# Modulation sums as rows in four column quarters, and a prologue with the first weights behind the first chunk

## The chip, the cores and the metric

The kernel runs on one core of one Trainium2 chip. The metric is the device time of one execution in microseconds. TensorE multiplies, VectorE, ScalarE and GpSimd do the elementwise work, and SyncE issues the DMAs. The inputs are float32.

## What is computed

One sample of 512 latent tokens and 256 context tokens, width 1024, goes through two layers. Each layer is half a gated FFN, a mixer (pooling and neighbourhood attention in layer 0, a gated recurrence in layer 1), and half a gated FFN again. Each block's input is normalised and modulated by shift and scale, and its output by a gate. These modulations are one vector of 9 x 1024 for each layer, and they come from a matrix of 1024 x 9216:

```
mx = (silu(c) @ ada_w[i] + ada_b[i])        # for x
mc = (silu(c_ctx) @ ada_w[i] + ada_b[i])    # for the context
x = x + 0.5 * mx[2] * swiglu(modulate(rms_norm(x, norm_g[i, 0]), mx[0], mx[1]),
                             ffn_w_gu[i, 0], ffn_w_down[i, 0])
...                                         # mixer with mx[3..5], second FFN with mx[6..8]
def modulate(h, shift, scale): return h * (1.0 + scale) + shift
def swiglu(h, w_gu, w_down):
    u = h @ w_gu
    return (silu(u[..., :D_FF]) * u[..., D_FF:]) @ w_down      # D_FF = 2816
```

## The kernel before

**Panels.** All activations lie transposed in SBUF, 128 channels on the partitions and T = 768 tokens along the columns. A product goes panel by panel: a panel is 128 output channels, its weights are 8 k-tiles of 128 x 128 (11 in the down products). Each weight and activation is split in a high and a low part; a k-tile is three products of 768 columns, run as six matmuls of 384 columns. SyncE loads a panel to `raw`, ScalarE rounds it to `w_hi` (`high`, L802), GpSimd subtracts it to `w_lo` (`low`, L691), TensorE multiplies (`panel`, L1661). There are two buffers of each, by the panel's parity, and two PSUM pairs, `pA` (pair_a) and `pB` (pair_b). Semaphores tie the engines: `raw_landed`, `hi_done`, `split_ready`, `panel_used`.

**FFN stages.** A stage `gu{f}{h}` makes the gate and the up panel of 11 channel tiles, in tiles of two panels: ScalarE takes SiLU of the gate (L809), VectorE multiplies by the up product (L1136) and splits the result (L1139, L1142). A stage `dn{f}{h}` makes 8 panels in pairs, each added to the residual by VectorE (L1167, `update`). f counts the four FFNs, h their halves. Where a norm follows (dn01, dn11, dn21, dn31), the last two panels are done in halves of the tokens (`tail`), so that the norm's row sums can start.

**Modulation.** The 9216 columns of a layer are cut in pieces of 256, numbered q, two channel tiles t each. Pieces 0 to 7 (shift and scale of the first norm) are made in the prologue. Pieces 8 to 71 are made one by one beside the FFN panels of f = 0 and 1 and of stage dn20: one piece for each tile of a gu stage, one for each pair of a dn stage, 64 in all. For a piece, SyncE loads 1 MB (`load_ada`), VectorE multiplies its 8 k-tiles by the vectors c and c_ctx, one number for each partition (v = 0, 1), and adds them up (`sum_ada`, L1102 and L1106: 16 instructions). What remains is a sum over the 128 partitions. TensorE does it in `use_ada`:

```
for t in range(2):
    for v in range(2):
        last = nc.tensor.matmul(pC[:, 2 * t + v:2 * t + v + 1], ada_sum[:, v, t * P:(t + 1) * P],
                                ones[:, 0:1], start=True, stop=True)
```

The sums are the stationary operand and a column of ones is moved. VectorE then adds the bias to the four columns (`take_ada`, L1120), which gives `mods`.

**Prologue.** SyncE loads x, the context, the small vectors and four chunks of 2 MB of `ada_w` (`load_ada0`; 2 and 0 are the tiles 0 to 3 of scale and shift, 3 and 1 the tiles 4 to 7). TensorE turns x, multiplies each chunk by c with the channels of `cvec_pad` as four stationary quarters of 32 columns (`ada_rows`, L1836), ScalarE copies the rows out (L940), TensorE turns them (`turn_ada`, L1844), and VectorE adds the bias (L1330). After chunks 2 and 0 VectorE and ScalarE make the normalised rows k = 0 to 3 for both halves of the tokens (`scale_rows` L1234, `high_rows` L863, `low_rows` L1245), after chunks 3 and 1 the rows k = 4 to 7. `first_panels` (L1651 to L1653) then makes panels 0 and 1 in the order: pair_a half 0, pair_b half 0, pair_a half 1, pair_b half 1, each over all eight k.

The order on each engine is the order of the code; the values waited for are written out by hand.

## Time and profile before

| what | us |
|---|---|
| median of the three runs (lowest to highest) | 2862.66 (2860.46 to 2863.76) |
| time of the profiled execution | 2863.28 |
| its span, first to last instruction | 2861.3 |
| TensorE busy | 2705.3 (95%) |
| TensorE weight loads busy | 2545.7 (89%) |
| VectorE, ScalarE, GpSimd busy | 1458.5, 783.1, 895.3 |

The profile shows one execution; an engine's busy time is the union of its instructions. A matmul's end is modelled: it is shown as longer than the distance to the next one. Where matmuls follow each other, the distance from start to start is what one costs; where one group of them ends and another begins, the start of the group's last is its end less the length of one.

### The profile page before, as it was taken

The page shows a single profiled execution, that of the slowest core. Times are in us where ns is not written, and L with a number is a line of the kernel's source. Part 1 is how long each engine was busy: PE and PEld are TensorE (multiplying, and loading weights), DVE is VectorE, ACT ScalarE, POOL GpSimd, SP SyncE. Part 2 cuts the span into 40 slices and gives each one's busy share as a digit, 9 for nine tenths or more (in the row PEclk, how much of TensorE's full clock was granted, in tenths as well). Part 3 has the DMA queues.
Part 4 walks back from the last instruction along what each step waited for, and adds up shares of the span by engine and source line. Part 5 has one row for each costly group of instructions (what it writes and reads, how often), then busy time and mean ns, then how long its engine had stood idle before and what let it go on. Part 6 is the DMA issues. An engine that isn't in the chain of part 4 may idle for free.

```text
span 2861.3 us, 40076 instructions
## 1 busy us (share of the span) xinstructions
PE 2705.3 (95%) x15097; PEld 2545.7 (89%) x15097; DVE 1458.5 (51%) x2525; ACT 783.1 (27%) x1053; POOL 895.3 (31%) x365
## 2 busy tenths in 40 slices
PE   5999999999989899999999999999998887899998
PEld 4899999998957899999999999999997775778887
DVE  5565456655463656645666323422247886432233
ACT  3221122212164322111112322111225664332222
POOL 0332232322232223322222223223223443344442
...
GB/s 201 118 117 131 96 108 122 128 83 71 106 35 22 74 115 120 112 102 120 122 109 89 52 66 95 82 66 61 73 46 52 48 48 66 63 95 103 88 104 80
DMA packets 413084, 256.78 MB, mean 90 GB/s; under 512 B 6653, under 2 KB 405846, under 8 KB 413014
## 3 DMA queue, kind: packets, MB, share of 16 engines
...
q14 instruction: 29, 0.24, 0.0%
...
## 4 chain that ended last, share of the span: by engine, by line
PE 53%; issue 28%; DVE 8%; POOL 7%; ACT 4%; DMA 0%; POOLq 0%; SPq 0%; DVEq 0%; ACTq 0%
PE pair_b L1661 24%; PE pair_a L1661 23%; POOL w_lo L691 7%; PE pair_c L1711 1%; DVE decay L1621 1%; DVE h_lo L1245 1%; DVE ada_sums L1106 1%; DVE decay L1619 1%; DVE gate_i L1615 1%; DVE root L1613 1%; ACT decay L1044 1%; ACT root L1046 1%; PE pair_a L1651 1%; PE pair_r L1955 1%; PE pair_c L1937 1%
## 5 line engine op out<-in xcount | busy, mean ns | idle before, releaser
L691 POOL TENSOR_TENSOR w_lo<-raw,w_hi 128x1024 fp32r<-128x1024 f32 (+3 forms) x302 | 827.2, 2740 | 1764.2 <-ACT w_hi L802 1764.2
L802 ACT ACTIVATE w_hi<-raw 128x1024 fp32r<-128x1024 f32 (+3 forms) x302 | 337.2, 1117 | 1284.2 <-PE pair_b L1661 447.5
L1136 DVE TENSOR_TENSOR work_g<-work_s,pair_b 128x768 f32<-128x768 f32 (+1 forms) x88 | 78.1, 888 | 690.2 <-PE pair_b L1661 526.6
L1106 DVE SCALAR_TENSOR_TENSOR ada_sums<-ada_raw,cvec,ada_sums 128x256 f32<-128x256 f32 x896 | 400.0, 519 | 0.0
L1661 PE MATMUL pair_a<-h_hi,w_hi 128*128 128x384 f32 x1312 | 339.8, 339 | 12.7 <-POOL w_lo L691 12.7
L1661 PE MATMUL pair_a<-h_lo,w_hi 128*128 128x384 f32 x1312 | 334.5, 335 | 0.0
L1661 PE MATMUL pair_a<-h_hi,w_lo 128*128 128x384 f32 x1312 | 334.1, 335 | 0.0
L1661 PE MATMUL pair_b<-h_hi,w_hi 128*128 128x384 f32 x1168 | 298.2, 336 | 10.5 <-POOL w_lo L691 10.5
L1661 PE MATMUL pair_b<-h_lo,w_hi 128*128 128x384 f32 x1168 | 297.6, 335 | 0.0
L1661 PE MATMUL pair_b<-h_hi,w_lo 128*128 128x384 f32 x1168 | 297.3, 335 | 0.0
L1661 PEld LDWEIGHTS pair_a<-h_hi,w_hi 128*128 128x128 f32 x1312 | 235.5, 189 | 17.0 <-issue 8.6
L1661 PEld LDWEIGHTS pair_a<-h_lo,w_hi 128*128 128x128 f32 x1312 | 238.5, 189 | 0.0
L1661 PEld LDWEIGHTS pair_a<-h_hi,w_lo 128*128 128x128 f32 x1312 | 238.0, 189 | 0.0
L1661 PEld LDWEIGHTS pair_b<-h_hi,w_hi 128*128 128x128 f32 x1168 | 211.4, 188 | 11.4 <-POOL w_lo L691 11.4
L1661 PEld LDWEIGHTS pair_b<-h_lo,w_hi 128*128 128x128 f32 x1168 | 211.9, 189 | 0.0
L1661 PEld LDWEIGHTS pair_b<-h_hi,w_lo 128*128 128x128 f32 x1168 | 211.9, 189 | 0.0
L1167 DVE SCALAR_TENSOR_TENSOR resid<-pair_b,mod_g,resid 128x512 f32<-128x512 f32 (+3 forms) x74 | 42.2, 602 | 314.5 <-PE pair_b L1661 245.3
L1651 PE MATMUL pair_b<-h_hi,w_hi 128*128 128x512 f32 (+3 forms) x352 | 140.1, 398 | 32.0 <-DVE gelu L1600 31.8
L1142 DVE TENSOR_TENSOR g_lo<-work_g,g_hi 128x768 f32 (+1 forms) x88 | 155.6, 1768 | 10.8
L1652 PE MATMUL pair_b<-h_lo,w_hi 128*128 128x512 f32 (+3 forms) x352 | 138.1, 392 | 0.0
L1653 PE MATMUL pair_b<-h_hi,w_lo 128*128 128x512 f32 (+3 forms) x352 | 137.3, 390 | 0.0
L1651 PE MATMUL pair_a<-h_hi,w_hi 128*128 128x512 f32 (+2 forms) x280 | 113.4, 405 | 20.7 <-DVE h_lo L1245 16.9
...
## 6 DMA issues: line engine op xcount, KB each, us to landing
...
ada_first<-in_ada_w_dram SPq DMA_DIRECT2D x4, 2048.0 KB, 15.0
...
```

The source lines that it names most:

```text
L691: nc.gpsimd.tensor_tensor(wl[:, par, 0:kt * P], raw[:, par, 0:kt * P], wh[:, par, 0:kt * P].bitcast(F32), ALU.subtract).then_inc(split_rea ...
L802: nc.scalar.activation(wh[:, par, 0:kt * P], raw[:, par, 0:kt * P], ACT.Copy).then_inc(hi_done, 1)
L1044: nc.scalar.activation(decay[d][:, :], gate_r[d][:, :], ACT.Exp, bias=rg_scale[:, m:m + 1], scale=rg_scale[:, m:m + 1])
L1046: nc.scalar.activation(root[d][:, :], gate_r[d][:, :], ACT.Tanh, bias=rg_tanh[:, m:m + 1], scale=rg_tanh[:, m:m + 1]).then_inc(decay_done, 1)
L1106: step = nc.vector.scalar_tensor_tensor(out=sums[v], in0=tiles(k), scalar=c_k, in1=sums[v], op0=ALU.mult, op1=ALU.add)
L1136: nc.vector.tensor_tensor(gbuf[:, 0, 0:W], sbuf[:, 0, 0:W], up, ALU.mult)\
L1142: nc.vector.tensor_tensor(gl[:, ds(i, 1), 0:W].rearrange("p o n -> p (o n)"), gbuf[:, 0, 0:W], gh[:, ds(i, 1), 0:W].rearrange("p o n -> p ...
L1167: return nc.vector.scalar_tensor_tensor(out=resid[:, k, a:b], in0=src, scalar=mod_g[:, SITE[name], k, v:v + 1], in1=resid[:, k, a:b], op0= ...
L1651: nc.tensor.matmul(dst, w1, hi, start=start, stop=False)
L1652: nc.tensor.matmul(dst, w1, lo, start=False, stop=False)
L1653: return nc.tensor.matmul(dst, w2, hi, start=False, stop=stop)
L1661: last = nc.tensor.matmul(tokens(ps, a, a + HALF), w, of[:, k, a:a + HALF], start=begins, stop=ends)
```

## The change

**Modulation sums.** TensorE now keeps a 32 x 128 block of PSUM for each of the four (t, v), in the four quarters of pC's partitions. For a piece, VectorE copies 32 columns of `one_hot` (zero but for one column of ones) to `row_hot`, so that the one stands at the piece's place in its group. `use_ada` then takes `row_hot` (32 columns) as the stationary operand and moves the sums (128 columns), which adds the piece's row to the block. Pieces are gathered in six groups (`GROUPS_AT`) of 11, 15, 4, 11, 15 and 8. `begin_group` clears the blocks by four products with zero weights. When a group is whole, VectorE copies the blocks to SBUF (`copy_group`), TensorE transposes them (`turn_group`) and VectorE adds the bias of the whole group (`take_group`). Four groups are turned within the first pair of the next dn stage, one at the end of dn01's tail, one behind dn20's last panel.

**Prologue.** The weights of panels 0 and 1 are loaded behind chunk 2 and split early; GpSimd no longer waits for the rows k = 0 to 3. Chunk 3's rows are copied after half 0 and chunk 1's after row k = 1 of half 1. `opening_panels` makes panels 0 and 1 in the order: for k = 0 to 3, half 0 of pair_a and pair_b, half 1 of both; then the same for k = 4 to 7. Chunk 1's product stands behind the first eight k-tiles, its turn behind the next four.

```
+        GROUPS_AT = [[("gu00", KC)], [("dn00", KD // 2), ("gu01", KC)], [("dn01", KD // 2)], [("gu10", KC)],
+                     [("dn10", KD // 2), ("gu11", KC)], [("dn11", KD // 2), ("dn20", KD // 2)]]
+        GROUP_OF, GROUP_FIRST, GROUP_SIZE = {}, [], []
+        for g, parts in enumerate(GROUPS_AT):
+            GROUP_FIRST.append(ada_first[parts[0][0]])
+            GROUP_SIZE.append(sum(n for _, n in parts))
+            for part, _ in parts:
+                GROUP_OF[part] = g
+        TURNED_IN = {"dn00": 0, "dn01": 1, "dn10": 3, "dn11": 4}
...
-            load_ada0(2)
-            load_ada0(0)
-            load_ada0(3)
                     if p0 == 0:
+                        load_ada0(2)
                         load(0, 0, KD, gu[:, :, 0:P])
                         load(1, 1, KD, gu[:, :, DFF:DFF + P])
+                        load_ada0(0)
+                        load_ada0(3)
                         load_ada0(1)
...
+            nc.gpsimd.memset(one_hot[:, :], 0.0).then_inc(const_done, 1)
+            pool.wait_ge(const_done, 4)
+            nc.gpsimd.memset(one_hot[:, QUAD - 1:QUAD], 1.0).then_inc(const_done, 1)
-            pool.wait_ge(h_ready, KD)
             ffn(0)
...
             copy_ada0(0, pR, 512)
+            high(0)
+            high(1)
             for half in range(2):
                 root_half("in", half)
             copy_ada0(1, pB, 0)
...
             for half in range(2):
                 for k in range(4):
                     high_rows("in", half, k)
-            copy_ada0(2, pB, 512)
-            high(0)
-            high(1)
-            copy_ada0(3, pA, 0)
+                    if half == 1 and k == 1:
+                        copy_ada0(3, pC, 512)
+                if half == 0:
+                    copy_ada0(2, pB, 512)
             act.wait_ge(coef_done, 2)
...
-            def sum_ada(q):
+            def sum_ada(q, name):
 
                 dve.wait_ge(ada_landed, (q - (ADA0 - 1)) * 16)
+                dve.wait_ge(ada_used, q - (ADA0 - 1))
+                nc.vector.tensor_copy(row_hot[:, :], one_hot[:, ds(q - GROUP_FIRST[GROUP_OF[name]], QUAD)]).then_inc(row_chosen, 1)
                 sum_tiles(lambda k: ada_raw[:, k, :], [ada_sum[:, v, :] for v in range(2)], ada_summed, sums_before(q))
 
-            def take_ada(q):
-
-                dve.wait_ge(ada_used, q - (ADA0 - 2))
-                src = pC[:, 0:4].rearrange("p (t v) -> p v t", v=2)
+            def copy_group(g):
+
+                dve.wait_ge(ada_used, ada_seen(GROUP_FIRST[g] + GROUP_SIZE[g] - 1))
+                nc.vector.tensor_copy(mod_rows[:, :], pC[:, 0:P]).then_inc(group_copied, 1)
+
+            def take_group(g):
+
+                q, n = GROUP_FIRST[g], GROUP_SIZE[g]
+                dve.wait_ge(group_turned, g + 1)
+                turned = pC[:, 640:640 + P].rearrange("p (t v j) -> p v t j", v=2, j=QUAD)[:, :, :, QUAD - n:QUAD]
                 for v in range(2):
-                    last = nc.vector.tensor_tensor(mods[:, ds(q * 2, 2), v], src[:, v, :], cols[:, ds(q * 2, 2)], ALU.add)
-                last.then_inc(mods_done, 1)
+                    last = nc.vector.tensor_tensor(mods[:, 2 * q:2 * (q + n), v].rearrange("p (j t) -> p t j", t=2),
+                                                   turned[:, v, :, ::-1],
+                                                   cols[:, 2 * q:2 * (q + n)].rearrange("p (j t) -> p t j", t=2), ALU.add)
+                last.then_inc(mods_done, n)
...
+                if name in TURNED_IN:
+                    sum_ada(q0, name)
+                    copy_group(TURNED_IN[name])
+                    take_group(TURNED_IN[name])
...
+                if name == "dn20":
+                    copy_group(5)
+                    take_group(5)
...
+            def opening_panels(between):
+
+                p = first["gu00"]
+                for ks in (range(4), range(4, KD)):
+                    for half in range(2):
+                        a, b = half_of("in", half)
+                        for r in range(2):
+                            pe.wait_ge(split_ready, p + r + 1)
+                            for k in ks:
+                                pe.wait_ge(h_ready, row_number(0, half, k) + 1)
+                                last = passes(tokens(pair[r], a, b), r, k, hh[:, k, a:b], hl[:, k, a:b], k == 0, k == KD - 1)
+                            if k == KD - 1 and half == 1:
+                                last.then_inc(panel_used, 1)
+                            between(ks[0], half, r)
+
+            def begin_group(g):
+
+                if g == 0:
+                    pe.wait_ge(const_done, 5)
+                else:
+                    pe.wait_ge(group_copied, g)
+                for c in range(4):
+                    nc.tensor.matmul(pC[c * QUAD:(c + 1) * QUAD, 0:P], one_hot[:, QUAD:2 * QUAD], ident[:, :], start=True,
+                                     stop=False, skip_group_check=True)
+
+            def turn_group(g):
+
+                pe.wait_ge(group_copied, g + 1)
+                if g >= 1:
+                    pe.wait_ge(mods_done, ada_seen(GROUP_FIRST[g] - 1))
+                nc.tensor.transpose(pC[:, 640:640 + P], mod_rows[:, :], ident[:, :]).then_inc(group_turned, 1)
+
+            def use_ada(q, name):
 
                 pe.wait_ge(ada_summed, sums_before(q + 1))
-                pe.wait_ge(mods_done, q - (ADA0 - 1))
+                pe.wait_ge(row_chosen, q - (ADA0 - 1))
                 for t in range(2):
                     for v in range(2):
-                        last = nc.tensor.matmul(pC[:, 2 * t + v:2 * t + v + 1], ada_sum[:, v, t * P:(t + 1) * P],
-                                                ones[:, 0:1], start=True, stop=True)
+                        c = 2 * t + v
+                        last = nc.tensor.matmul(pC[c * QUAD:(c + 1) * QUAD, 0:P], row_hot[:, :], ada_sum[:, v, t * P:(t + 1) * P],
+                                                start=False, stop=False, skip_group_check=True)
                 last.then_inc(ada_used, 1)
...
+                        if opening and r == 0:
+                            if name in TURNED_IN:
+                                turn_group(TURNED_IN[name])
+                            if name in GROUP_OF and ada_first[name] == GROUP_FIRST[GROUP_OF[name]]:
+                                begin_group(GROUP_OF[name])
                         if q0 is not None and r == 0:
-                            use_ada(i + q0)
+                            use_ada(i + q0, name)
+
+                if name in TURNED_IN:
+                    two(0, True)
+                    start = 1
+                with pe.Fori(start, KD // 2 - int(name in NORM_AT)) as i:
+                    two(i)
+                if name == "dn20":
+                    turn_group(5)
...
             turn_ada(2, KD + 4)
-            ada_rows(1, pA[:, 0:512])
-            turn_ada(3, 4).then_inc(ada_used, 1)
+
+            def modulation_ends(k0, half, r):
+
+                if (k0, half, r) == (0, 0, 1):
+                    ada_rows(1, pC[:, 512:1024])
+                elif (k0, half, r) == (0, 1, 0):
+                    turn_ada(3, 4).then_inc(ada_used, 1)
+
             pe.wait_ge(cols_done, 1)
             ffn(0, "in")
```

TensorE in the prologue before, from chunk 3's turn to the first rows of panel 0. L1844 is a chunk's turn, L1836 a chunk's product, L1651 to L1653 the three products of a k-tile:

```order
L1844 MATMUL pair_c<-quad_sums,ada_first_rows 128x2 [waits ada0_copied,mods_first]
L1844 MATMUL pair_c<-quad_sums,ada_first_rows 128x2 x3
L1836 MATMUL pair_a<-ada_first,cvec_padded 32x512 [waits ada0_landed1]
L1836 MATMUL pair_a<-ada_first,cvec_padded 32x512 x7
L1844 MATMUL pair_c<-quad_sums,ada_first_rows 128x2 [waits ada0_copied]
L1844 MATMUL pair_c<-quad_sums,ada_first_rows 128x2 x3
L1651 MATMUL pair_a<-h_hi,w_hi 128x384 [waits h_ready,split_ready,cols_done]
L1652 MATMUL pair_a<-h_lo,w_hi 128x384
L1653 MATMUL pair_a<-h_hi,w_lo 128x384
L1651 MATMUL pair_a<-h_hi,w_hi 128x384 [waits h_ready]
L1652 MATMUL pair_a<-h_lo,w_hi 128x384
```

And of the change, from chunk 3's product (L1926) on; L1934 is a turn, L1686 to L1688 a k-tile:

```order
L1926 MATMUL pair_b<-ada_first,cvec_padded 32x512 [waits ada0_landed3]
L1926 MATMUL pair_b<-ada_first,cvec_padded 32x512 x7
L1934 MATMUL pair_c<-quad_sums,ada_first_rows 128x2 [waits ada0_copied,mods_first]
L1934 MATMUL pair_c<-quad_sums,ada_first_rows 128x2 x3
L1686 MATMUL pair_a<-h_hi,w_hi 128x384 [waits h_ready,split_ready,cols_done]
L1687 MATMUL pair_a<-h_lo,w_hi 128x384
L1688 MATMUL pair_a<-h_hi,w_lo 128x384
```

Chunk 3's turn is now followed by panel 0 at once. Chunk 1's product stands further on in the change, behind the k-tiles 0 to 3 of half 0 of both panels:

```order
L1686 MATMUL pair_b<-h_hi,w_hi 128x384 [waits h_ready]
L1687 MATMUL pair_b<-h_lo,w_hi 128x384
L1688 MATMUL pair_b<-h_hi,w_lo 128x384
L1926 MATMUL pair_c<-ada_first,cvec_padded 32x512 [waits ada0_landed1]
L1926 MATMUL pair_c<-ada_first,cvec_padded 32x512 x7
L1686 MATMUL pair_a<-h_hi,w_hi 128x384 [waits h_ready,split_ready]
```

And its turn stands behind the k-tiles 0 to 3 of half 1 of panel 0:

```order
L1686 MATMUL pair_a<-h_hi,w_hi 128x384 [waits h_ready]
L1687 MATMUL pair_a<-h_lo,w_hi 128x384
L1688 MATMUL pair_a<-h_hi,w_lo 128x384
L1934 MATMUL pair_c<-quad_sums,ada_first_rows 128x2 [waits ada0_copied]
L1934 MATMUL pair_c<-quad_sums,ada_first_rows 128x2 x3
L1686 MATMUL pair_b<-h_hi,w_hi 128x384 [waits h_ready,split_ready]
```

Both have moved from ahead of the panels to between their pieces.

ScalarE in the prologue before, from row k = 3 of half 1 on. L863 is a rounded row, L940 the copy of a chunk's rows, L802 the rounding of a panel's weights:

```order
L863 ACTIVATE h_hi<-work_g,mods 128x128 [waits scaled_done]
L863 ACTIVATE h_hi<-work_g,mods 128x256
L863 ACTIVATE h_hi<-work_g,mods 128x128 [waits scaled_done]
L863 ACTIVATE h_hi<-work_g,mods 128x256
L940 ACTIVATE ada_first_rows<-pair_b 128x512 [waits ada0_mm]
L802 ACTIVATE w_hi<-raw 128x1024 [waits raw_landed0]
L802 ACTIVATE w_hi<-raw 128x1024 [waits raw_landed1]
L940 ACTIVATE ada_first_rows<-pair_a 128x512 [waits ada0_mm]
L863 ACTIVATE h_hi<-work_s,mods 128x384 [waits scaled_done,coef_done]
```

And of the change, from the first chunk's copy (L959) to that of chunk 3; L821 rounds weights, L874 is the norm's root, L882 a rounded row:

```order
L959 ACTIVATE ada_first_rows<-pair_r 128x512 [waits ada0_mm]
L821 ACTIVATE w_hi<-raw 128x1024 [waits raw_landed0]
L821 ACTIVATE w_hi<-raw 128x1024 [waits raw_landed1]
L874 ACTIVATE std<-mean_sq 128x3 [waits ms_done] x2
L959 ACTIVATE ada_first_rows<-pair_b 128x512 [waits ada0_mm]
L882 ACTIVATE h_hi<-work_s,mods 128x384 [waits scaled_done,coef_first]
L882 ACTIVATE h_hi<-work_s,mods 128x384 [waits scaled_done]
L882 ACTIVATE h_hi<-work_g,mods 128x384 [waits scaled_done] x2
L959 ACTIVATE ada_first_rows<-pair_b 128x512 [waits ada0_mm]
```

A little further on, in half 1, the copy of chunk 1 (into which pair_c goes) stands between the rows k = 1 and k = 2:

```order
L882 ACTIVATE h_hi<-work_s,mods 128x128 [waits scaled_done]
L882 ACTIVATE h_hi<-work_s,mods 128x256
L959 ACTIVATE ada_first_rows<-pair_c 128x512 [waits ada0_mm]
L882 ACTIVATE h_hi<-work_g,mods 128x128 [waits scaled_done]
L882 ACTIVATE h_hi<-work_g,mods 128x256
```

The weights are rounded ahead of the norm's root, and both copies moved in among the rows of the first four k.

TensorE at the end of tile 1 of stage gu00 before: the end of the up panel, the sums of a piece (L1711), the loop and the next gate panel:

```order
L1661 MATMUL pair_b<-h_hi,w_lo 128x384 x2
L1711 MATMUL pair_c<-ones,ada_sums 128x1 [waits mods_done,ada_summed]
L1711 MATMUL pair_c<-ones,ada_sums 128x1 x3
L1745 UNCONDITIONAL_BRANCH
L1745 ISA
L1722 REGISTER_ALU [waits split_ready]
L1661 MATMUL pair_a<-h_hi,w_hi 128x384 [waits silu_done]
```

And of the change in the middle of the same tile, where a group begins (L1761) and a piece is taken (L1778):

```order
L1696 MATMUL pair_a<-h_hi,w_lo 128x384 x2
L1761 MATMUL pair_c<-ident,one_hot 32x128 [waits const_done]
L1761 MATMUL pair_c<-ident,one_hot 32x128 x3
L1778 MATMUL pair_c<-ada_sums,row_hot 32x128 [waits row_chosen,ada_summed]
L1778 MATMUL pair_c<-ada_sums,row_hot 32x128 x3
L1696 MATMUL pair_b<-h_hi,w_hi 128x384 [waits gate_up_done,split_ready]
```

The four products of a piece have 32 stationary columns and move 128, where they had 128 and moved 1; they wait for `row_chosen` where they waited for `mods_done`.

VectorE at the beginning of stage dn00, of the change (before, L1092's `mod_g` stood first, then the sums, and L1120 after each piece):

```order
L1135 COPY row_hot<-one_hot 128x32 [waits ada_used,ada_landed]
L1123 TENSOR_SCALAR ada_sums<-ada_raw,cvec 128x256 x2
L1127 SCALAR_TENSOR_TENSOR ada_sums<-ada_raw,cvec,ada_sums 128x256 [waits ada_summed] x14
L1141 COPY mod_rows<-pair_c 128x128 [waits ada_used]
L1149 TENSOR_TENSOR mods<-pair_c,cols 128x2x11 [waits group_turned]
L1149 TENSOR_TENSOR mods<-pair_c,cols 128x2x11
L1113 TENSOR_SCALAR mod_g<-mods 128x16 [waits mods_done]
L1196 SCALAR_TENSOR_TENSOR resid<-pair_a,mod_g,resid 128x512 [waits panel_used,coef_done]
```

The copy of the blocks, the bias of the group and `mod_g` moved behind the sums of the stage's first piece.

## Rows read from the trace of the kernel before

**Rows 1.** Page, first part: busy us (share of the span) x instructions.

```profile
PE 2705.3 (95%) x15097; PEld 2545.7 (89%) x15097; DVE 1458.5 (51%) x2525; ACT 783.1 (27%) x1053; POOL 895.3 (31%) x365
```

**Rows 2.** Timeline of ScalarE: start and length us, line, operation, count, [idle before].

```profile
132.64 0.81 ACT L809 ACTIVATE work_s<-pair_a 128x768 f32<-128x768 f32 x1
150.18 0.81 ACT L809 ACTIVATE work_s<-pair_a 128x768 f32<-128x768 f32 x1
1618.85 0.81 ACT L809 ACTIVATE work_s<-pair_a 128x768 f32<-128x768 f32 x1
1635.49 0.81 ACT L809 ACTIVATE work_s<-pair_a 128x768 f32<-128x768 f32 x1
```

**Rows 3.** Timeline of TensorE round one use of modulation sums.

```profile
139.06 0.51 PE L1661 MATMUL pair_b<-h_hi,w_lo 128*128 128x384 f32 x2
139.41 0.95 PE L1711 MATMUL pair_c<-ones,ada_sums 128*128 128x1 f32 x8
140.22 0.59 PE L1661 MATMUL pair_a<-h_hi,w_hi 128*128 128x384 f32 x2
```

**Rows 4.** Modulation sums on TensorE: ns min/median/max; who it waited for.

```profile
L1711 PE MATMUL pair_c<-ones,ada_sums x512: 165/250/271, 88.1 to 1843.0; 128*128 128x1 f32 x171
  DVE ada_sums L1106: 3.3, 5
```

**Rows 5.** Attention's values: one instruction (ns), TensorE's timeline round their beginning and end.

```profile
L1955 PE MATMUL pair_r<-prob_t,v_tokens x192: 272/273/421, 816.9 to 892.6; 128*64 128x128 f32 x192
819.24 0.66 PE L1937 MATMUL pair_c<-ident,prob 128*128 128x128 f32 x4 [0.23 <-DVE prob L1532]
819.83 0.55 PE L1955 MATMUL pair_r<-prob_t,v_slabs 128*64 128x128 f32 x6
892.25 0.66 PE L1955 MATMUL pair_r<-prob_t,v_tokens 128*64 128x128 f32 x8 [0.82 <-ACT prob_t L903]
892.84 0.62 PE L1661 MATMUL pair_a<-h_hi,w_hi 128*128 128x384 f32 x2
893.29 0.35 PE L1661 MATMUL pair_a<-h_lo,w_hi 128*128 128x384 f32 x1
```

**Rows 6.** Timeline of the prologue: TensorE.

```profile
24.80 1.92 PE L1836 MATMUL pair_r<-ada_first,cvec_padded 128*32 128x512 f32 x16
41.01 3.28 PE L1836 MATMUL pair_b<-ada_first,cvec_padded 128*32 128x512 f32 x16
59.24 0.42 PE L1651 MATMUL pair_a<-h_hi,w_hi 128*128 128x384 f32 x1
```

**Rows 7.** Timeline of the prologue: ScalarE and VectorE.

```profile
45.26 0.61 ACT L863 ACTIVATE h_hi<-work_g,mods 128x384 fp32r<-128x384 f32 x1 [0.44 <-DVE work_g L1234]
59.42 0.24 DVE L1330 TENSOR_TENSOR mods<-pair_c,cols 128x8 f32<-128x8 f32 x2 [7.06 <-PE pair_c L1844]
74.09 1.28 ACT L809 ACT_TABLE_LOAD   x1 [4.21 <-PE pair_a L1653]
```

**Rows 8.** Stretches: length, busy us by engine, clock, DMA share, GB/s.

```profile
30.00:43.00 13.00, 13.00 (x64) 8.60 (x68) 3.55 (x16) 1.63 (x5) 0.00 (x0) 0.51 0.80 268
47.50:57.00 9.50, 4.80 (x24) 2.37 (x24) 4.43 (x13) 5.17 (x11) 3.85 (x2) 0.50 0.01 3
```

**Rows 9.** TensorE's first rows of tile 1 in stage gu00.

```profile
79.64 0.62 PE L1661 MATMUL pair_a<-h_hi,w_hi 128*128 128x384 f32 x2 [1.49 <-POOL w_lo L691]
```

**Rows 10.** Chunk 2: its issue on SyncE's queue; KB and us to landing.

```profile
6.32 8.35 SPq L511 DMA_DIRECT2D ada_first<-in_ada_w_dram  x3
ada_first<-in_ada_w_dram SPq DMA_DIRECT2D x1, 2048.0 KB, 11.9
```

**Rows 11.** Stage dn00, first pair: VectorE, TensorE. Stage dn20: last update.

```profile
268.79 5.62 DVE L1106 SCALAR_TENSOR_TENSOR ada_sums<-ada_raw,cvec,ada_sums 128x256 f32<-128x256 f32 x14
274.48 1.04 PE L1711 MATMUL pair_c<-ones,ada_sums 128*128 128x1 f32 x8
1854.88 1.14 DVE L1167 SCALAR_TENSOR_TENSOR resid<-pair_b,mod_g,resid 128x512 f32<-128x512 f32 x2 [11.06 <-PE pair_b L1661]
```

56 lines of the change are left out of this document (33 added, 23 removed).

## The prediction

> **What bounds the kernel now.** I began with the busy shares: TensorE is busy 95% of the span, every other engine at most half of it [rows 1]. So what counts is what TensorE executes and where it waits. Next I took the distance from one SiLU of ScalarE to the next, which is the time of one tile of a gate and up stage. With a modulation piece in the tile it is 150.18 - 132.64 = 17.54 us, without one 1635.49 - 1618.85 = 16.64 us [rows 2]. The difference, 0.90 us, is what one piece costs. The timeline says where: eight instructions of TensorE between two panels [rows 3], 512 in all for 64 pieces, and TensorE waited for VectorE's sums only 5 times, 3.3 us together [rows 4]. So the pieces cost 64 x 0.90 = 57.6 us of TensorE's own time, nearly all of it on the path that sets the end. The second place is the prologue, where TensorE first multiplies a k-tile of panel 0 at 59.24 us [rows 6], while VectorE and ScalarE had the first rows long before.
>
> **A piece, before and after.** Before: eight loads of 128 stationary columns, and the next two k-tile products take a little longer to get going. After: four quarter products of 32 stationary and 128 moved columns. The trace of before has no such product, so I build the cost from its neighbours. Four quarters run abreast: 16 instructions of 512 columns took 1.92 us [rows 6], that is four rounds of 0.43 us and the end of the last. A piece of the change is eight instructions of 128 columns, two rounds. What a round of 128 columns costs, and what it costs to go from full products to part products and back, the attention's values show [rows 5] (halves of 64 columns there, not quarters; I take them as equal). In: the transposes begin at 819.24 and their last ends at 819.90; one lasts 0.27, so the last began at 819.63, and the first half product at 819.83, 0.20 later. Some 0.11 of this is the transpose's own 128 columns, 0.09 the change. A k-tile product of 384 columns takes 0.17 by itself (16.64 / 96), so 0.26 from its start to the first quarter. Rounds: eight instructions, four rounds, from 892.25 to 892.64 (end less 0.27): 0.39 for three distances; the first is about 0.16, the others 0.11. Out: from the last at 892.64 to the full product at 892.84, 0.20. The first two full products then take 0.45 where two are 0.35. Together, over what TensorE would need without a piece: (0.26 - 0.17) + 0.16 + 0.02 (stagger of four) + 0.20 + 0.10 = 0.57 us. A piece saves 0.90 - 0.57 = 0.33 us. Bounds: 0.22 if the two changes cost nothing, below; 0.75 if four quarters cost twice what two halves do at both changes.
>
> The Trainium skill has a rule that speaks against the change: "TensorEngine Tiling (Array Packing)", Key Properties, says that changing the tiling mode drains TensorE. By that rule each piece pays two drains; the page gives no time for one, and the trace agrees, with about 0.09 us at each change.
>
> I count 62 pieces; the first two lie in the prologue's shift, below. 62 x 0.33 = **20.5 us less**.
>
> **What the groups add.** (1) Six times `begin_group`, two more rounds in the same mode, 0.22 us; five count: +1.1. (2) Four groups are turned behind the first panel of a dn stage. The turn waits for VectorE's copy, and that now stands behind the sums of the stage's first piece. In dn00 these sums ended at 268.79 + 5.62 = 274.41, TensorE began the piece at 274.48 [rows 11]: no slack at all. In the change TensorE is there 0.33 earlier, VectorE has `row_hot` more (0.1), then the copy of 128 columns from PSUM (0.2) and two hand-overs (0.1 to 0.2). TensorE waits about 0.7, and the transpose is 0.2. Four times 0.9: +3.6. Queued behind the turn is the second panel of the pair. `mod_g` and the first update come about 1.3 us later than before; the panel that needs the buffer begins 11.4 us after, so nobody waits. (3) Behind dn20's last panel TensorE turns group 5. Ahead of VectorE's copy stands the update of that very panel, 1.14 us [rows 11]. With copy, hand-overs and transpose +1.9, where gu21 used to start at once. (4) The group turned at the end of dn01's tail: TensorE waits there for the norm's rows anyway, +0.2. (5) VectorE's `row_hot` copy, 64 times 0.1 us. In the gate and up tiles VectorE waits for the up panel, so it is hidden; in dn01 and dn11, where the sums came last, I add +0.6. What goes are 2 small additions a piece (0.22 us) which nobody waited for. Sum: **+7.4 us**.
>
> **The prologue.** Weights first: chunk 2 was issued at 6.32 and landed 11.9 later, at 18.2 [rows 10]. The 1 MB of weights behind it lands at about 22 even at the slow 268 GB/s of [rows 8], well before ScalarE has finished the squares; chunk 0 comes some 3 us later, which TensorE doesn't notice. GpSimd's two subtractions fall beside VectorE's statistics, which have over 2 us to spare. On TensorE chunk 3's product ends at 41.01 + 3.28 = 44.3 [rows 6]. ScalarE ends row k = 3 of half 0 at 45.26 + 0.61 = 45.9 [rows 7] and copies chunk 3's rows at once, 0.6; the turn then takes 1.0 to 1.8, so panel 0 begins at about 47.6 where it began at 59.24. But TensorE soon needs what isn't there. 24 products of half 0 take 4.2 us at full clock and 7.7 at half; the granted clock was 0.50 from 47.5 to 57, with TensorE half idle [rows 8]. I take half clock until about 51, so 53.4. Chunk 1's product takes 1.9: 55.3. ScalarE stands still from about 48.7 for this copy, then makes rows k = 2 and 3 of half 1, so half 1 of panel 0 ends only at 58.9, and the turn at 59.9. Before, VectorE took that turn at 59.42 [rows 7]: the second four rows start no earlier, 0.5 later. They set the end: by the old pace panel 0's last k-tile comes at 71.7, and panel 1's at 73.8. Before, panel 0 ended when ScalarE loaded its table, 74.09 [rows 7]. And that is the hand that counts, since SiLU, the rounding of panel 2's weights and GpSimd's subtraction hang on panel 0: tile 1 began at 79.64, after waiting for GpSimd [rows 9]. So not the 4 us that TensorE's own end moves by, but 74.1 - 71.7 = 2.4 are passed on, with 0.2 for the first pieces: **-2.6 us**. Bounds: 0.5 more than before (the later turn, if panel 0 waits too) and -4.4 (full clock throughout).
>
> **Sum.** -20.5 + 7.4 - 2.6 = -15.7. The profiled execution took 2863.3 us, 2.0 more than its span; the change gives 2847.6 there. The median of the runs is 0.6 lower, so 2847.0.
>
> **Rivals.** (A) Slower: the change between full and quarter products is dearer than between full and half ones. The sum turns positive when a piece costs over 0.90 - 4.8 / 62 = 0.82 us, a quarter of a microsecond more than I take. At 1.0 us it is 62 x 0.1 + 4.8 = +11: 2874. Against it: every one of the attention's changes that I looked at stands at 0.20. Chance 0.05. (B) Changing costs nothing and a piece is its two rounds, 0.22 us: 62 x 0.68 = 42.2 less, 2826. Against it stand the same rows. The same page of the Trainium skill, Theoretical Speedup, gives up to 4 times for 32 columns, which would also be 0.90 / 4 = 0.22. Chance 0.05. (C) In the dn stages VectorE becomes the last: its slack was 0.07 us in dn00's first pair [rows 11], and it gets the copy of `row_hot` and sometimes a GpSimd subtraction between. Then the 24 pieces there save nothing: +7.9, 2855. Chance 0.17. (D) The prologue gives nothing, because ScalarE, stopped at chunk 1's copy, holds back the rows, and panel 0 ends as before or later: 2850 to 2853. Chance 0.12. (E) More: full clock in the prologue and cheaper turns, 2834 to 2841. Chance 0.08. (F) The forecast as it stands, 2841 to 2852: 0.53.
>
> **The numbers.** 2847.0. A measurement of this kernel can tell about 0.2%, 5.7 us, from no change: below 2857.0 is faster, above 2868.4 slower. B, C, D, E and F lie below 2857 with most of their width, that is 0.83 for faster, 0.09 for the same, and 0.08 for slower (A and the worst of C). The range takes in C, D and most of E: 2838 to 2858.
>
> **What would show it.** A tile of a gate and up stage with a piece should take 17.2 us; 17.4 or more speaks for A, 16.9 for B. A pair of a dn stage should take 0.33 less too; if TensorE waits for the sums there, it is C. The idle time before the transposes should be 0.7 four times and about 1.5 behind dn20. In the prologue panel 0 should begin at 47 to 48, ScalarE's first SiLU table load should stand at about 71.7, and tile 1 at 77.2. The prediction fails if quarter products keep the panel's weights from being loaded for longer than half products do.

## The result and the profile after

The changed kernel takes 2844.6 us (median of 4 runs, 2844.3 to 2845.5), the kernel before, on the same chip, 2862.0 (4 runs). The ratio is 0.994, with a 95% interval of 0.9928 to 0.9953: faster by 0.6%, 17.4 us by the medians. The profiled execution took 2844.3 us with a span of 2842.5, where the one before had 2861.3: 18.8 us less. The forecast was 2847.

The first reading is again the distance between two SiLUs. The timeline of ScalarE in stage gu00 of the changed kernel (start and length in us, line, operation) answers to [rows 2], TensorE's round one piece to [rows 3]:

```profile
130.37 0.82 ACT L828 ACTIVATE work_s<-pair_a 128x768 f32<-128x768 f32 x1
147.59 0.82 ACT L828 ACTIVATE work_s<-pair_a 128x768 f32<-128x768 f32 x1
...
136.79 0.51 PE L1696 MATMUL pair_b<-h_hi,w_lo 128*128 128x384 f32 x2
137.23 0.43 PE L1778 MATMUL pair_c<-ada_sums,row_hot 128*32 128x128 f32 x8
137.58 0.62 PE L1696 MATMUL pair_a<-h_hi,w_hi 128*128 128x384 f32 x2
```

A tile with a piece takes 17.22 us, 0.32 less than before; from the last two full products to the next it is 0.79 where it was 1.16. In gu20, which has no pieces, a tile takes 16.64 in both kernels.

TensorE's waits in the changed kernel (who waited for whom: us in total, times, longest), and one line of the same view of the kernel before, which was not shown ahead of the prediction:

```profile
PE pair_b L1696 <- POOL w_lo L711: 8.4, 3, 3.0
PE pair_c L1769 <- DVE mod_rows L1141: 2.3, 5, 1.4
```
```profile
PE pair_b L1661 <- POOL w_lo L691: 10.5, 3, 4.2
```

The second line is the five turns. The other two are a wait that the prediction didn't speak of: three times TensorE stands before the second panel of a tile, until GpSimd has made its low part.

The prologue of the changed kernel, all engines (the answer to [rows 6, 7, 9]), and two stretches round the start of tile 1 (length, busy us by engine, granted clock, DMA):

```profile
44.95 1.14 PE L1934 MATMUL pair_c<-quad_sums,ada_first_rows 128*128 128x2 f32 x8 [3.57 <-ACT ada_first_rows L959]
53.74 0.60 ACT L959 ACTIVATE ada_first_rows<-pair_c 128x512 f32<-128x512 f32 x1 [6.59 <-PE pair_c L1926]
58.18 0.24 DVE L1364 TENSOR_TENSOR mods<-pair_c,cols 128x8 f32<-128x8 f32 x2 [1.67 <-PE pair_c L1934]
69.97 5.63 DVE L1127 SCALAR_TENSOR_TENSOR ada_sums<-ada_raw,cvec,ada_sums 128x256 f32<-128x256 f32 x14
70.39 1.28 ACT L828 ACT_TABLE_LOAD   x1 [1.73 <-PE pair_a L1688]
73.52 4.28 POOL L711 TENSOR_TENSOR w_lo<-raw,w_hi 128x1024 fp32r<-128x1024 f32 x1 [38.73 <-ACT w_hi L821]
77.85 1.01 PE L1696 MATMUL pair_a<-h_hi,w_hi 128*128 128x384 f32 x2 [5.48 <-POOL w_lo L711]
```
```profile
77.00:81.00 4.00, 3.15 (x10) 3.15 (x11) 2.17 (x2) 0.00 (x0) 0.80 (x1) 0.50 1.02 325
77.85:83.00 5.15, 5.15 (x16) 5.15 (x17) 1.32 (x2) 0.07 (x1) 0.00 (x0) 0.50 1.15 333
```

Everything up to the table load is near the forecast or ahead of it: 70.39 where 71.7 was predicted and 74.09 stood before. But tile 1 begins only 1.8 us sooner than before, after an idle time of 5.48 us where it was 1.49 [rows 9], and then runs at half clock (0.50) for over 5 us. When ScalarE rounds panel 4, nothing is left:

```profile
90.34 1.05 ACT L802 ACTIVATE w_hi<-raw 128x1024 fp32r<-128x1024 f32 x1
```
```profile
91.02 1.06 ACT L821 ACTIVATE w_hi<-raw 128x1024 fp32r<-128x1024 f32 x1
```

That is before, then after. So three questions went to the chip: does the prologue give anything, is it the quarters abreast that pay, and what are the three waits for GpSimd.

### The profile page after: what moved, and what is told of

Read it like the earlier page. It is cut to its first block, busy times and chain, and to the rows that moved or that the text cites. A ratio compares the mean times of both kernels' runs of the same rounds, so it can differ in the third digit from the quotient of the medians.

```text
span 2842.5 us, 40073 instructions
## 1 busy us (share of the span) xinstructions
PE 2685.2 (94%) x15151; PEld 2498.1 (88%) x15151; DVE 1461.2 (51%) x2479; ACT 784.8 (28%) x1053; POOL 905.6 (32%) x367
## 4 chain that ended last, share of the span: by engine, by line
PE 51%; issue 29%; DVE 8%; POOL 7%; ACT 4%; DMA 0%; POOLq 0%; SPq 0%; DVEq 0%; ACTq 0%
PE pair_b L1696 24%; PE pair_a L1696 22%; POOL w_lo L711 7%; DVE ada_sums L1127 1%; DVE decay L1656 1%; DVE decay L1654 1%; DVE h_lo L1278 1%; DVE gate_i L1650 1%; DVE root L1648 1%; ACT decay L1065 1%; ACT root L1067 1%; PE pair_r L2051 1%; PE pair_c L2033 1%; PE pair_c L1778 1%; PE pair_a L1686 0%
## 5 line engine op out<-in xcount | busy, mean ns | idle before, releaser
L711 POOL TENSOR_TENSOR w_lo<-raw,w_hi 128x1024 fp32r<-128x1024 f32 (+3 forms) x302 | 837.4, 2774 | 1733.4 <-ACT w_hi L821 1733.4
L821 ACT ACTIVATE w_hi<-raw 128x1024 fp32r<-128x1024 f32 (+3 forms) x302 | 337.6, 1118 | 1279.3 <-PE pair_b L1696 440.6
L1696 PE MATMUL pair_a<-h_hi,w_hi 128*128 128x384 f32 x1312 | 340.6, 340 | 17.6 <-POOL w_lo L711 17.4
L1696 PE MATMUL pair_a<-h_lo,w_hi 128*128 128x384 f32 x1312 | 335.1, 336 | 0.0
L1696 PE MATMUL pair_a<-h_hi,w_lo 128*128 128x384 f32 x1312 | 334.4, 335 | 0.0
L1696 PE MATMUL pair_b<-h_hi,w_hi 128*128 128x384 f32 x1168 | 298.3, 336 | 8.4 <-POOL w_lo L711 8.4
L1696 PE MATMUL pair_b<-h_hi,w_lo 128*128 128x384 f32 x1168 | 297.5, 335 | 0.0
L1696 PE MATMUL pair_b<-h_lo,w_hi 128*128 128x384 f32 x1168 | 297.3, 335 | 0.0
L1696 PEld LDWEIGHTS pair_a<-h_hi,w_hi 128*128 128x128 f32 x1312 | 234.6, 189 | 30.0 <-issue 16.3
L1696 PEld LDWEIGHTS pair_a<-h_lo,w_hi 128*128 128x128 f32 x1312 | 238.4, 189 | 0.0
L1696 PEld LDWEIGHTS pair_a<-h_hi,w_lo 128*128 128x128 f32 x1312 | 238.2, 189 | 0.0
L1696 PEld LDWEIGHTS pair_b<-h_hi,w_hi 128*128 128x128 f32 x1168 | 211.5, 189 | 9.8 <-POOL w_lo L711 9.4
L1696 PEld LDWEIGHTS pair_b<-h_lo,w_hi 128*128 128x128 f32 x1168 | 211.8, 189 | 0.0
L1696 PEld LDWEIGHTS pair_b<-h_hi,w_lo 128*128 128x128 f32 x1168 | 211.7, 188 | 0.0
L1686 PE MATMUL pair_b<-h_hi,w_hi 128*128 128x512 f32 (+3 forms) x352 | 139.0, 395 | 33.7 <-DVE gelu L1635 33.5
L1173 DVE TENSOR_TENSOR g_lo<-work_g,g_hi 128x768 f32 (+1 forms) x88 | 136.0, 1545 | 10.8
L1688 PE MATMUL pair_b<-h_hi,w_lo 128*128 128x512 f32 (+3 forms) x352 | 136.1, 387 | 0.0
L1686 PE MATMUL pair_a<-h_hi,w_hi 128*128 128x512 f32 (+2 forms) x280 | 114.9, 410 | 21.1 <-DVE h_lo L1278 17.4
## 6 DMA issues: line engine op xcount, KB each, us to landing
ada_first<-in_ada_w_dram SPq DMA_DIRECT2D x4, 2048.0 KB, 13.5
```

The costliest lines, as they stand in the source:

```text
L711: nc.gpsimd.tensor_tensor(wl[:, par, 0:kt * P], raw[:, par, 0:kt * P], wh[:, par, 0:kt * P].bitcast(F32), ALU.subtract).then_inc(split_rea ...
L821: nc.scalar.activation(wh[:, par, 0:kt * P], raw[:, par, 0:kt * P], ACT.Copy).then_inc(hi_done, 1)
L1173: nc.vector.tensor_tensor(gl[:, ds(i, 1), 0:W].rearrange("p o n -> p (o n)"), gbuf[:, 0, 0:W], gh[:, ds(i, 1), 0:W].rearrange("p o n -> p ...
L1686: nc.tensor.matmul(dst, w1, hi, start=start, stop=False)
L1688: return nc.tensor.matmul(dst, w2, hi, start=False, stop=stop)
L1696: last = nc.tensor.matmul(tokens(ps, a, a + HALF), w, of[:, k, a:a + HALF], start=begins, stop=ends)
```

## Experiments

Ratios are to the kernel before on the same chip. Offsets between two traces are read at the same panel's rounding, since the rg stage, which no edit touches, varies by up to 4 us between executions.

### The two halves of the change by themselves

`sums_only`, in the prologue:

```diff
-                    if after == "in":
-                        opening_panels(modulation_ends)
-                    else:
-                        first_panels(p0, after, W, W)
+                    first_panels(p0, after, W, W)
```

with the loads, ScalarE's order and TensorE's turns of before. `prologue_only` is the reverse: those four places as changed, `use_ada`, `take_ada` and `sum_ada` as before.

> Only the modulation sums are changed (quarter products, groups); the prologue is that of the kernel before. Theory: the sums carry nearly the whole gain: 62 or more pieces at 0.33 us, less the groups' costs of 5.5 us as the trace of the change shows them (begin 0.22 each, turns 0.55 four times, 2.06 behind dn20), so 15 to 16 us less than before, about 2846.5, and a gu tile of 17.2 us. Rival: the prologue gave half of it by what hangs on it later; then this stays above 2853.

> Only the prologue is changed; the sums are those of the kernel before. Theory: panel 2's rounding comes 3.7 us earlier, but tile 1 only 1.8 us and the later tiles about 2, since GpSimd's subtraction of panel 2 meets VectorE's sums of piece 8; so 2 us less than before, about 2860. Rival: the 3.7 us are passed on whole, 2858.3; second rival: nothing arrives, 2862.

Measured: `sums_only` 2844.1 us, ratio 0.9939 (0.9926 to 0.9953), the same as the whole change, and 2.4 us below its theory's 2846.5. `prologue_only` 2863.9 (11 runs, 2859.2 to 2867.9), ratio 1.001 (1.0001 to 1.0019): no gain, if anything a small loss, so its theory of 2 us less falls. The whole gain is the sums'; the term of -2.6 for the prologue falls.

### Four products one after another

```diff
-                        last = nc.tensor.matmul(pC[c * QUAD:(c + 1) * QUAD, 0:P], row_hot[:, :], ...
+                        last = nc.tensor.matmul(pC[0:WIDE, c * P:(c + 1) * P], row_hot[:, :], ...
```

`WIDE` is 72, so no product lies in a quarter and none runs beside another; the rest of the change stands.

> As the change, but the four products of a piece have 72 stationary columns and go to four column blocks of pair_c one after the other, not to four quarters abreast; the blocks' rows 0 to 31 are copied at a group's end with four copies. Theory: what the change gains is that the four products run abreast, at the price of two changes of mode. Without both a piece is eight instructions of 128 moved columns at 0.11 us, 0.88 to 0.95 us again, a gu tile 17.5 us, and the whole 62 x 0.33 = 20 us above the change, about 2865. Rival: the gain comes from the shorter stationary loads (72 columns against 128) and the change of mode eats the rest; then a piece stays near 0.6 us and the whole near 2847.

Measured: 2879.3 us, ratio 1.0061 (1.0047 to 1.0075). ScalarE's and TensorE's timelines in `full_width`:

```profile
133.09 0.81 ACT L828 ACTIVATE work_s<-pair_a 128x768 f32<-128x768 f32 x1
150.64 0.81 ACT L828 ACTIVATE work_s<-pair_a 128x768 f32<-128x768 f32 x1
...
139.86 1.04 PE L1780 MATMUL pair_c<-ada_sums,row_hot 128*72 128x128 f32 x8
```

A tile takes 17.55 us: the piece costs 0.91, as before the change. So products of 128 columns in place of single ones are no gain; that four of them run abreast is. The rival (the shorter stationary operand is the gain) would have 0.6 us for a piece, and falls. From the first product of the piece to the next full product it is 0.79 us here and 0.35 in the change; since eight moves of 128 columns fill the 0.79, only overlap brings them to 0.35. The total is 14 us above the theory's 2865. Over the change it is 34.7 us: some 21 from the pieces, 3.3 from the turns (5.6 us of waits where the change has 2.3), 4.8 from the three waits for GpSimd (13.2 in all, where the change has 8.4). About 6 us are not assigned here.

### The copy of the group ahead of the next sums

```diff
-                    sum_ada(q0, name)
                     copy_group(TURNED_IN[name])
+                    sum_ada(q0, name)
                     take_group(TURNED_IN[name])
```

and in dn20 the copy ahead of the last update.

> As the change, but VectorE copies a group's blocks ahead of the sums of the dn stage's first piece, and group 5's blocks ahead of the update of dn20's last panel. Theory: the waits ahead of the five transposes (0.3 to 0.4 four times, 1.6 behind dn20, 2.9 us together) are the copy's place in VectorE's queue and go: about 2841.7, with TensorE waiting under 0.1 us there. Rival: TensorE then waits for the sums of the piece instead, and only the 1.6 behind dn20 goes: 2843.

Measured: 2840.9 us, ratio 0.993 (0.9916 to 0.9944), but with two outcomes: 2840.0, 2840.7 and 2840.9, and 2846.3 and 2846.9. The interval overlaps that of the change (0.9928 to 0.9953), so by time alone the gain of 3.8 us is not shown. The trace speaks for it: no wait for `mod_rows` is left, those for the sums stay small (2.3 us where they were 2.1), and against the changed kernel the rounding of the panels moves ahead by 0.4 us at each of four turns and by 2.0 behind dn20, 3.6 together. The trace is of the slow outcome, and it loses mostly at one place, tile 1 of stage gu10, where the wait for GpSimd is 7.0 us instead of 2.9. VectorE's sums, GpSimd's subtraction of panel 88's weights beside them, and the next issues on SyncE's queue; first the changed kernel, then `copies_first`:

```profile
995.87 5.63 DVE L1127 SCALAR_TENSOR_TENSOR ada_sums<-ada_raw,cvec,ada_sums 128x256 f32<-128x256 f32 x14
997.67 6.08 POOL L711 TENSOR_TENSOR w_lo<-raw,w_hi 128x1024 fp32r<-128x1024 f32 x1 [4.88 <-ACT w_hi L821]
1001.69 0.37 SPq L542 DMA_DIRECT2D ada_raw<-in_ada_w_dram  x1
1002.32 1.99 SPq L535 DMA_DIRECT2D raw<-in_ffn_w_gu_dram  x2
```
```profile
995.18 7.77 DVE L1127 SCALAR_TENSOR_TENSOR ada_sums<-ada_raw,cvec,ada_sums 128x256 f32<-128x256 f32 x14
996.98 2.52 POOL L711 TENSOR_TENSOR w_lo<-raw,w_hi 128x1024 fp32r<-128x1024 f32 x1 [5.06 <-ACT w_hi L821]
1003.15 0.37 SPq L542 DMA_DIRECT2D ada_raw<-in_ada_w_dram  x1
1003.78 1.61 SPq L535 DMA_DIRECT2D raw<-in_ffn_w_gu_dram  x2
```

Read the second column: either VectorE's fourteen sums take 5.63 us and GpSimd's subtraction is drawn out to 6.08, or the subtraction takes its 2.5 and the sums take 7.77. In both the subtraction begins 1.80 us after the sums, so the order of starts doesn't decide it here. The two engines shut each other out, and one of them pays.

Elsewhere the offset does decide. In the fourteen traces a subtraction begins beside these sums 308 times. In all 231 in which it begins up to 1.2 us after the first of the fourteen, GpSimd keeps its pace; in all 64 in which it begins 1.9 us or more after it, VectorE does; in the 13 between, nearly all at 1.8, GpSimd wins 4 times and VectorE 9. In the kernel before, the same place has 1.12 us, and GpSimd wins:

```profile
1005.23 7.76 DVE L1106 SCALAR_TENSOR_TENSOR ada_sums<-ada_raw,cvec,ada_sums 128x256 f32<-128x256 f32 x14
1006.35 2.40 POOL L691 TENSOR_TENSOR w_lo<-raw,w_hi 128x1024 fp32r<-128x1024 f32 x1 [4.67 <-ACT w_hi L802]
```

In the changed kernel TensorE is done with the piece sooner and no additions (L1120) stand ahead of the sums, so VectorE begins them some 0.7 us earlier: 1.8 us instead of 1.1, from where GpSimd always wins to where either may. In `full_width`, where TensorE takes longer again over the piece, this place has 0.64 us, and GpSimd wins (its 2.49 us beside a chain of 7.77).

The Trainium skill, "SBUF — State Buffer", section "SBUF: two separate sides", calls their shared port pair an exclusive lock which the loser waits for in full, a VectorE operation with two SBUF inputs being one that takes it. The trace agrees that they exclude each other. It agrees on VectorE as the loser, too: one of the fourteen takes 2.62 us where the others take 0.48. It differs for GpSimd, which as the loser waits through all that is left of the chain (6.08 us, of which some 2.4 are its own).

The last two lines show who pays in the end: SyncE issues the next piece 0.19 us after the sums end, and the weights of the tile's second panel stand behind it in the queue.

### The weights ahead of the piece

```diff
                         load(i * 2 + p0, 0, KD, gu[:, :, span(i * P + h * KC * P, P)])
-                        between()
                         load(i * 2 + (p0 + 1), 1, KD, gu[:, :, span(i * P + (DFF + h * KC * P), P)])
+                        between()
```

`between()` issues the piece's load. The edit was made to the kernel before, to the changed one, and to the one with the prologue alone.

> The kernel before with one line moved: in the gate and up stages SyncE issues the second weight panel of a tile ahead of the next modulation piece, where before the piece stood between the two panels and its issue waited for VectorE's sixteen sums of the last piece. Theory (the held queue): the three waits of TensorE for GpSimd's subtraction of a tile's second panel in the opening tiles of gu00, gu01 and gu10 (4.2 us the longest, 10.5 us in all in the trace of the kernel before) come from a weight load that stands behind the piece, whose issue waits for the sums; they vanish, and the time falls by 8 to 12 us, to about 2851. Rival (the piece comes late instead): the piece's own load is now behind a weight load, VectorE's sums start later, and TensorE waits for them in each of 44 tiles; the time rises above 2865.

> The same move of one line on the changed kernel, whose three waits of this kind are 8.4 us in all. Theory (the held queue): they vanish, 7 to 10 us less, about 2836, and the repeated runs lie within 2 us of one another. Rival (these waits are covered by others: GpSimd's subtraction of the next panel is late for another reason): within 2 us of the changed kernel, 2843 to 2846.

> The kernel with the new prologue alone, with the same line moved. Beside the kernel before with the line moved it prices the prologue where the queue no longer stands behind the first piece's sums. Theory (the prologue's 3.4 us at the rounding of panel 2 were lost since panel 3's load stood behind the sums, which ended only 0.9 us sooner): of the 3.4 us at least 1.5 come through, so 1.5 to 3 us under the run of the kernel before with the line moved. Rival (they are lost at the start of tile 1, to GpSimd's subtraction under VectorE's sums, 4.2 us where it took 2.4, and to the half clock behind the longer wait): within 1 us of that run.

Measured: on the kernel before 2847.3 us, ratio 0.9948 (0.9934 to 0.9961), 13.5 less than before; on the changed one 2832.5, ratio 0.9898 (0.9883 to 0.9913), 12.1 less than the change by the medians. The wait of `pair_b` for `w_lo` in L1661 and L1696 is gone from both lists. In `before_weights_first` VectorE loses in gu10 as it did before, and this costs TensorE 0.71 us at the sums, which it cost there too, but no longer the wait of 4.2 behind them:

```profile
996.53 7.76 DVE L1106 SCALAR_TENSOR_TENSOR ada_sums<-ada_raw,cvec,ada_sums 128x256 f32<-128x256 f32 x14
997.65 2.40 POOL L691 TENSOR_TENSOR w_lo<-raw,w_hi 128x1024 fp32r<-128x1024 f32 x1 [10.80 <-ACT w_hi L802]
1004.35 1.05 PE L1711 MATMUL pair_c<-ones,ada_sums 128*128 128x1 f32 x8 [0.71 <-DVE ada_sums L1106]
```

The held queue is what turns 2 us of VectorE into 4 to 7 us of TensorE. Both rivals fall. The gain is more than the waits (13.5 for 10.5, 12.1 for 8.4), since behind such a wait TensorE also ran at a lower clock for a while. In the kernel before, the stretch behind the wait of 4.2 in gu00:

```profile
112.00:116.00 4.00, 4.00 (x15) 4.00 (x16) 0.00 (x0) 0.00 (x0) 2.15 (x1) 0.57 1.13 341
```

The rounding of the panels moves ahead by 6.0 us there, 4.2 of wait and some 1.8 of clock. What didn't come true is that the repeated runs lie close together: `after_weights_first` has 2831.0 to 2835.7, where 2 us were expected, and `before_weights_first` 2842.9 to 2851.1. The held queue is thus not what spreads the runs, or not alone. One moved line thus gives three quarters of what the whole change gives.

With the prologue alone it is 2850.5 us (ratio 0.9966, 0.9952 to 0.998), 3.2 more than `before_weights_first`. The runs of the two overlap (2847.0 to 2854.0 and 2842.9 to 2851.1), so a loss isn't shown, but my theory of 1.5 to 3 us less falls too: the prologue gives nothing with a free queue either.

### Who holds tile 1

Each run's first pieces of the trace shift by up to 3.7 us as a whole: VectorE's first addition to `mods` lies between 37.8 and 41.6 in runs with the same prologue. So I count from VectorE's second addition, 59.42 before and 58.18 after. Tile 1 starts 20.2 us behind it in the kernel before, `sums_only` and `before_weights_first`, and 19.6 or 19.7 in every run with the new prologue so far. In each of the latter GpSimd's subtraction ends 2.2 us behind VectorE's sixteen sums: it takes 4.2 us, being shut out till they are done. Three edits to `prologue_weights_first` move the parts of this chain. `round_first`:

```diff
+                if p0 == 0:
+                    high(2)
+                    silu(0, 0)
+                    high(3)
-                with act.Fori(0, KC - 1) as i:
+                with act.Fori(int(p0 == 0), KC - 1) as i:
```

`sums_behind`, in VectorE's tile 0 (the body of the loop is now `product`):

```diff
-                    sum_ada(i + q0)
                     product(i)
+                    sum_ada(i + q0)
```

`round_sums` has both.

> The new prologue alone with the weights ahead of the pieces, and ScalarE rounds panel 2 (and 3) of tile 1 around the first SiLU: panel 2 ahead of it, so that its rounding starts 2.1 us sooner (the table load of 1.28 and the SiLU of 0.81 us behind it). Counted from the second shift and scale rows (the second pair of additions that write mods), tile 1 starts at 19.6 us in every run with the new prologue so far. Theory (GpSimd's subtraction can't end before VectorE's sixteen sums do: it ended 2.2 us behind them in each run): tile 1 still starts at 19.6, and the time is that of the kernel it is built on, within 1 us by stage. Rival (the chain of rounding and subtraction sets it): tile 1 starts at 17.5.

> The new prologue alone with the weights ahead of the pieces, and in tile 0 VectorE takes the first piece's sixteen sums behind tile 0's product instead of ahead of it; ScalarE's order is untouched. Theory (tile 1 waits for GpSimd, which waits for the sums): the subtraction of panel 2 takes 2.4 instead of 4.2 us, and tile 1 starts at 17.7 to 17.9 us behind the second shift and scale rows instead of 19.6, with an idle time of 3.5 instead of 5.4 us. Rival (the subtraction is long for another reason, such as ScalarE's two roundings beside it): 19.6 as before.

> Both edits together. Theory: neither the sums nor the SiLU stand in the way; tile 1 starts at 15.8 us behind the second shift and scale rows, the idle time falls to about 1.6 us, the granted clock stays at 1.00 behind it, and panel 4 is rounded at about 26.5 us instead of 33.1; 1 to 2 us of that are given back where TensorE waits for the sums of the first two pieces, so 4 to 6 us in all. Rival (the sums come too late, and TensorE waits for them longer than it waited for GpSimd): panel 8 is rounded no sooner than 70.1 us behind those rows.

Measured: 2848.9, 2849.1 and 2852.4 us, ratios 0.9957 (0.9941 to 0.9974), 0.9956 (0.994 to 0.9973) and 0.9967 (0.9955 to 0.9978); none is told apart from `prologue_weights_first`. Tile 1 starts 19.6, 18.1 and 15.7 us behind the second addition. The sums, the subtraction and tile 1 in `round_first`, then the last two in `round_sums`, with its waits of that part:

```profile
68.33 5.62 DVE L1110 SCALAR_TENSOR_TENSOR ada_sums<-ada_raw,cvec,ada_sums 128x256 f32<-128x256 f32 x14
69.90 6.25 POOL L690 TENSOR_TENSOR w_lo<-raw,w_hi 128x1024 fp32r<-128x1024 f32 x1 [35.05 <-ACT w_hi L800]
76.21 1.01 PE L1665 MATMUL pair_a<-h_hi,w_hi 128*128 128x384 f32 x2 [5.40 <-POOL w_lo L690]
```
```profile
73.47 2.36 POOL L690 TENSOR_TENSOR w_lo<-raw,w_hi 128x1024 fp32r<-128x1024 f32 x1 [38.52 <-ACT w_hi L800]
75.88 0.62 PE L1676 MATMUL pair_a<-h_hi,w_hi 128*128 128x384 f32 x2 [1.50 <-POOL w_lo L690]
```
```profile
PE pair_c L1741 <- DVE ada_sums L1110: 4.1, 2, 2.3
```

`sums_behind` moves tile 1 by 1.5 us where 1.7 to 1.9 were expected; its subtraction takes 2.76 us. `round_first` is the cleanest: the rounding comes 2 us sooner, the subtraction takes 2 us longer (6.25, of which 2.4 is its own), and tile 1 doesn't move. With the sums out of the way and the rounding early, tile 1 starts 3.9 us sooner without a half clock, and then TensorE waits 4.1 us for those same sums; panel 8 is rounded at 70.3 us behind the second addition, where `prologue_weights_first` has 70.1. So the rival of `round_sums` holds, and the 4 to 6 us of its theory didn't come. Whichever of the two is put first, the opening is bound by VectorE: four rows, then sixteen sums.

### Chunk 1 early

```diff
             ada_rows(3, pB[:, 512:1024])
+            ada_rows(1, pC[:, 512:1024])
             pe.wait_ge(mods_first, 1)
             turn_ada(2, KD + 4)
+            turn_ada(3, 4).then_inc(ada_used, 1)
```

ScalarE copies chunk 1's rows behind chunk 3's; `opening_panels` has nothing between. This is the changed kernel otherwise, its queue held as ever.

> The changed kernel with chunk 1 taken right behind chunk 3: its product follows chunk 3's on TensorE, ScalarE copies both behind the first half's four rows, and both turns stand ahead of the opening panels, which then run without a break. SyncE's order is that of the changed kernel. VectorE's second four rows can start near 50 instead of 58 us and end near 63 instead of 69. Theory (what decides is when VectorE has made the rows and the first piece's sums, since the load of panel 3 stands behind them in SyncE's queue): the piece's issue moves from 75.8 to about 70, everything behind follows, and the time falls by 4 to 6 us, to about 2840. Rival (what decides is TensorE's own work on the opening panels and the loads): less than 1.5 us, 2843 to 2846.

Measured: 2838.0 us (2836.3 to 2842.4), ratio 0.9923 (0.9909 to 0.9937), 6.6 less than the change, a little more than the theory's 4 to 6. VectorE's second addition and tile 1:

```profile
50.60 0.23 DVE L1363 TENSOR_TENSOR mods<-pair_c,cols 128x8 f32<-128x8 f32 x2
...
70.25 1.01 PE L1695 MATMUL pair_a<-h_hi,w_hi 128*128 128x384 f32 x2 [5.17 <-POOL w_lo L711]
```

Both stand 7.6 us sooner than in the changed kernel, with the same 19.65 between them; at the later panels 6.0 to 6.3 of it are left. That is the prologue's missing lever: not when the panels begin, but when VectorE gets its second addition.

### The three edits together

> The changed kernel with the three edits that paid by themselves: the weights ahead of the piece in SyncE's queue (12.1 us under the changed kernel by medians), chunk 1 right behind chunk 3 (6.6 us), and VectorE's copy of the finished group ahead of the next piece's sums (3.8 us by medians). Theory (the three take different waits away: the queue behind the sums in three opening tiles, VectorE's second four rows in the prologue, TensorE's wait at a turn): they add up but for the part of the copies' and chunk 1's gain that came from the held queue, so 2820 to 2826 us. Rival (the first piece's sums bound the opening once more, and the early chunk 1 only lengthens the wait at tile 1): 2829 us or more.

Measured: 2821.4 us (2820.7 to 2822.0), ratio 0.986 (0.9843 to 0.9876). They add up: 12.1 + 6.6 + 3.8 = 22.5 under the change's 2844.6 would be 2822.1. Tile 1 again starts 19.65 us behind the second addition, so that bound stands and was only moved.

## Why the prediction was right, and where not

**A piece, 62 x 0.33.** Right. 17.54 - 17.22 = 0.32, and by its parts: 0.27 from the last full product to the first quarter (0.26 predicted), 0.20 from the last quarter to the next full product (0.20 predicted). 62 x 0.32 is 19.8 for the forecast 20.5. Rivals A and B (a dear change between full and quarter products, or a free one) fall, and `full_width` shows that being abreast is what counts.

**The groups, +7.4.** Too high. `begin_group` adds 0.24, where I put 0.22. The four turns in dn stages cost 0.49 to 0.59 each where I put 0.9, with idle times of 0.15 to 0.26 where I put 0.7: 2.2 for 3.6. In dn00 VectorE ended the copy at 270.01 and TensorE began the turn at 270.06; the hand-overs are shorter than I took them. Behind dn20 it is 2.1 for 1.9 (idle 1.4), behind dn01's tail 0.1 for 0.2. The +0.6 for late sums didn't come: these waits fell from 3.3 us [rows 4] to 2.1. In all about +4.3 (1.1 + 2.2 + 2.1 + 0.1 - 1.2). Rival C, VectorE as the last, came only at the turns. Its price was also misread: the dn stages have 20 pieces, not 24, so it would have been 6.6 us and not 7.9.

**The prologue, -2.6.** Wrong. That the prologue gives nothing is rival D's outcome, but it came neither by D's road (panel 0 did end sooner) nor at D's total of 2850 to 2853. What I said of ScalarE is in the trace: it stood still for 6.59 us before chunk 1's copy, the second addition came 18.61 us behind the first where it was 18.30 before, and panel 0's end moved as forecast (counted from the first addition the table load is 2.15 us sooner, for 2.4). The step that failed is "the hand that counts, since SiLU, the rounding of panel 2's weights and GpSimd's subtraction hang on panel 0". In the new order that hand is VectorE's: the subtraction now falls under the sums and can't end before them (`round_first`), so of 3.7 us at the table load tile 1 keeps 1.8, and 1.55 of that is the whole trace's earlier start: counted from the first addition tile 1 is 0.24 sooner. And I left out what the idle time costs: TensorE ends the opening panels 5.8 us sooner, stands still for 5.48 instead of 1.49 us, and comes back at a granted clock of 0.50 until about 83.1. I estimate that this costs 2.4 us: it starts 8.25 pairs of products in those 5.3 us, at 0.64 us a pair where 0.35 is usual. From the first addition to panel 4's rounding it is 51.45 us after and 49.22 before: the 0.24 gained less the 2.4.

**What I didn't see.** The queue. In tile 1 of gu00 and gu10 VectorE's sums lost to GpSimd's subtraction before and win in the changed kernel, and the three waits behind them fell from 10.5 to 8.4 us; that is 2.1 us of gain that no step of mine held. It belongs to the sums' half of the change, by the 0.7 us that VectorE is sooner: 8.3 in `sums_only`, 10.3 in `prologue_only`. Summed over the trace: -19.8 + 4.3 - 2.1, and +2.2 for the prologue, is -15.4 of the span's -18.8. Some 1.5 more are the earlier start of that execution (first addition at 39.57 against 41.12). That makes 16.9 of the 18.2 us by which the changed kernel is ahead where the rg stage begins; 1.3 are not assigned. In the untouched rg stage the lead grows to 20.6, and behind it 1.8 are lost again. So the forecast of -15.7 came close to the measured -17.4 by luck, by errors that cancel: groups 3 too dear, prologue 5 too cheap, the queue missing. What stays open is which of VectorE and GpSimd wins where the subtraction begins 1.8 us behind the sums, and what spreads the runs of `before_weights_first`.
